# Moving the stick-breaking attention beside the projections, and half of the output projection between the latent units

## The reference, cut to what matters

```python
h = rms_norm(x, g_pre_mix[i])
proj = h @ w_in[i]
sb_q, sb_k, sb_v, q_lat, kv_lat, k_rope = split(proj)
# stick-breaking: A = sigmoid(z) * prod of (1 - sigmoid(z)) over the keys between, 8 heads of 64
z = einsum('bhqd,bhkd->bhqk', q, k) * scale
log_keep = where(strict, -softplus(z), 0)
log_keep_after = cumsum(log_keep, reverse=True) - log_keep
o_sb = where(strict, exp(log_sigmoid(z) + log_keep_after), 0) @ v
# latent attention (MLA): 8 heads, queries and keys out of 256 and 128 latent features
q = rms_norm(q_lat, g_q_lat[i]) @ w_q_up[i];  kv = rms_norm(kv_lat, g_kv_lat[i]) @ w_kv_up[i]
o_mla = causal softmax attention of (q_nope, rope(q_rope)) on (k_nope, rope(k_rope)), v
mix = concatenate([rms_norm(o_sb, g_grp_sb[i]), rms_norm(o_mla, g_grp_mla[i])]) @ w_o[i]
x = x + rms_norm(mix, g_post_mix[i])
```

## Time and profile before

| | |
|---|---|
| median of three runs | 971.93 us |
| the profiled execution's own time | 972.83 us |
| its span | 971.1 us, 16923 instructions |
| TensorE busy | 893.0 us (92%) |
| VectorE, ScalarE, GpSimd busy | 689.6 (71%), 510.7 (53%), 320.6 us (33%) |
| DMA | 137.18 MB, mean 141 GB/s |
| the chain that ended last | TensorE 77%, VectorE 14%, issue 4%, ScalarE 4%, DMA 1% |

### The profile page before, as it was taken

The page is one execution under the profiler, slowest core; times in us unless marked ns, Lnnn a source line. Parts: engine busy times, 40 slices in busy tenths (PEclk is TensorE's granted clock), DMA queues, the critical chain, the costliest instruction groups (busy, mean ns, idle before and its releaser), DMA issues.

```text
span 971.1 us, 16923 instructions
## 1 busy us (share of the span) xinstructions
PE 893.0 (92%) x6718; PEld 850.5 (88%) x6718; DVE 689.6 (71%) x984; ACT 510.7 (53%) x926; POOL 320.6 (33%) x150
## 2 busy tenths in 40 slices
PE   4996779999999998889999489999996999999998
PEld 4985669999999998788989479988996999999998
DVE  6757742899889993768879998754677476566573
ACT  6377345654555556765756264446643544444441
POOL 4653103122233333253545451221343223223220
PEclk8997869999999998999999798899998999999999
DMA  5734004354565665361655242222354456656651
GB/s 190 280 112 150 22 2 115 107 181 149 168 206 177 204 183 154 91 191 62 208 158 166 111 152 66 87 87 66 101 161 130 125 159 197 187 176 184 189 153 44
DMA packets 54078, 137.18 MB, mean 141 GB/s; under 512 B 6000, under 2 KB 24816, under 8 KB 53872
## 3 DMA queue, kind: packets, MB, share of 16 engines
q1 hardware_dynamic: 54000, 136.11, 45.1%
HBM read 135.03 MB, written 1.05 MB: 140 GB/s over the span
## 4 chain that ended last, share of the span: by engine, by line
PE 77%; DVE 14%; issue 4%; ACT 4%; DMA 1%; SPq 0%; DVEq 0%; ACTq 0%
PE PROD L576 15%; PE PROD L577 14%; PE PROD L578 14%; PE SC L717 3%; PE OP L761 3%; DVE wlo L1491 3%; PE PROD L638 2%; PE OP L576 2%; PE OP L578 2%; PE OP L577 2%; PE SC L576 2%; PE SC L577 2%; PE SC L578 2%; PE TP L578 2%; PE TP L577 2%
## 5 line engine op out<-in xcount | busy, mean ns | idle before, releaser
L559 POOL TENSOR_TENSOR wlo<-raw,whi 128x1024 fp32r<-128x1024 f32 x124 | 316.7, 2561 | 626.8 <-ACT whi L1012 626.8
L576 PE MATMUL PROD<-HA,whi 128*128 128x256 f32 x1096 | 318.5, 291 | 10.4 <-DVE HA L1519 5.7
L577 PE MATMUL PROD<-HA,wlo 128*128 128x256 f32 x1096 | 314.3, 287 | 0.0
L578 PE MATMUL PROD<-HA,whi 128*128 128x256 f32 x1096 | 314.1, 287 | 0.0
L1012 ACT ACTIVATE whi<-raw 128x1024 fp32r<-128x1024 f32 x252 | 261.4, 1050 | 45.6 <-PE PROD L578 24.2
L1491 DVE TENSOR_TENSOR wlo<-raw,whi 128x1024 fp32r<-128x1024 f32 x128 | 183.1, 1434 | 102.9 <-ACT whi L1012 102.6
L576 PEld LDWEIGHTS PROD<-HA,whi 128*128 128x128 f32 x1096 | 214.8, 196 | 13.0 <-DVE HA L1519 6.1
L577 PEld LDWEIGHTS PROD<-HA,wlo 128*128 128x128 f32 x1096 | 214.9, 196 | 0.6 <-issue 0.6
L578 PEld LDWEIGHTS PROD<-HA,whi 128*128 128x128 f32 x1096 | 214.6, 196 | 0.0
L1906 DVE SCALAR_TENSOR_TENSOR CY<-U,CV,CY 128x255 f32<-128x255 f32 (+29 forms) x120 | 71.5, 670 | 0.2
L1773 DVE SCALAR_TENSOR_TENSOR YC<-Y,CV,YC 128x255 f32<-128x255 f32 x88 | 66.9, 763 | 2.2 <-ACT YC L1206 0.7
(11 more groups left out here) (316 smaller groups left out, 1707.7 us busy)
## 6 DMA issues: line engine op xcount, KB each, us to landing
raw<-stream SPq DMA_DIRECT2D x208, 512.0 KB, 3.9
raw<-stream SPq DMA_DIRECT2D x136, 128.0 KB, 2.4
raw<-stream SPq DMA_DIRECT2D x8, 384.0 KB, 3.1
raw<-stream SPq DMA_DIRECT2D x8, 256.0 KB, 3.3
X<-xT SPq DMA_DIRECT2D x2, 512.0 KB, 5.1
E<-memT SPq DMA_DIRECT2D x1, 1024.0 KB, 5.8
out<-X SPq DMA_DIRECT2D x8, 128.0 KB, 2.0
PX<-pT SPq DMA_DIRECT2D x1, 256.0 KB, 3.8
```

Source lines behind the costliest of these rows:

```text
L559: nc.gpsimd.tensor_tensor(wlo[:, n % NSPLIT, :], raw[:, n % NRAW, :], whi[:, n % NSPLIT, :].bitcast(F32), ALU.subtract).then_inc(lo_pool, 1)
L576: nc.tensor.matmul(dst, wh, hi, start=start, stop=False, skip_group_check=True)
L577: nc.tensor.matmul(dst, wl, hi, start=False, stop=False, skip_group_check=True)
L578: last = nc.tensor.matmul(dst, wh, lo, start=False, stop=stop, skip_group_check=True)
```

## The change

The first latent stage and its neighbours are put in another order.

- `mem` is loaded by two DMAs into `KMEM` and `VMEM` instead of one into `E0`, so that `E0` is free earlier.
- TensorE runs `sb_scores(0)` to `(2)` after `sbk` 1 to 3 and `sb_scores(3)` a quarter into `sbv`; `sb_cum` after every second `qup`; `sb_pv` behind it, the last one after `kup`. `scores(mla 0)` stands before `vup`. In the latent loop `scores(u+1)` stands before `turn(u)` and `pv(u)`.
- ACT runs the exponentials and logarithms of the stick-breaking units around the norm of `mem`, ahead of the splits of tiles 18 to 21. `token_root(osb)` stands between `exps(mla 0)` and `exps(mla 1)`.
- VectorE's stream follows this (`sb_scaled`, `softplus`, `sb_argument`, `rope_queries` are old code under names).
- The first six outputs of `wo` are computed in two halves: chunks 0 to 3 (the stick-breaking half) two outputs at a time after `pv` of latent units 1, 2 and 3, and chunks 4 to 7 after `turn_out(omla)`. Six outputs share the three banks, two in each, and the stream's order of blocks follows; each of these tiles is then loaded by two DMAs.

```diff
 for _n, _k, _m, _o in STAGES:
-    if _n in ("up", "up2"):
+    if _n == "wo":
+        for _h in (0, 4):
+            ORDER += [FIRST["wo"] + m * 8 + k for m in range(6) for k in range(_h, _h + 4)]
+        ORDER += range(FIRST["wo"] + 48, FIRST["wo"] + 64)
+    elif _n in ("up", "up2"):
...
+WO_HALVES = 6
...
     if _o[0] in ("down", "down2"):
         _k = 4 + _o[1] // 2
+    elif _o[0] == "wo" and _o[1] < WO_HALVES:
+        _k = _o[1] // 2
+        _seen[_k] = _i
+        PREV[_o] = _last.get(_k) if _o[1] % 2 == 0 else None
+        _last[_k] = _o
     else:
...
-T_USES = [("cum", 0)]
-for _u in range(1, 4):
-    T_USES += [("cum", _u), ("mla", _u - 1)]
-T_USES += [("mla", 3), ("osb", 0), ("omla", 0), ("mem", 0), ("mem", 1), ("omem", 0)]
+T_USES = [("cum", u) for u in range(4)] + [("mla", 0), ("osb", 0)] + [("mla", u) for u in range(1, 4)]
...
-O_USES = [("sb", 0), ("mla", 0), ("sb", 1), ("mla", 1), ("sb", 2), ("mla", 2), ("sb", 3), ("mla", 3)]
+O_USES = [("sb", u) for u in range(4)] + [("mla", u) for u in range(4)]
...
-        MEMX = E0[:, :, :].rearrange("p h n -> p (h n)")[:, 0:DC * S].rearrange("p (c s) -> p c s", c=DC)
+        MEMX = [KMEM[:, :, :], VMEM[:, :, :].rearrange("p q n -> p (q n)").rearrange("p (c s) -> p c s", c=4)]
...
+            if o[0] == "wo" and o[1] < WO_HALVES:
+                return PROD[:, k, o[1] % 2 * S:o[1] % 2 * S + S]
...
                 if n == 6:
-                    sp.dma_start(MEMX, memT).then_inc(mem_in, 16)
+                    for i in range(2):
+                        sp.dma_start(MEMX[i], memT[:, 4 * i:4 * i + 4, :]).then_inc(mem_in, 16)
...
             for m in range(4):
                 fm("sbk", m, HA)
+                if m:
+                    wait_freed(pe, ("sbk", m - 1))
+                    sb_scores(m - 1)
             stat("mem", [SQ[:, c, :] for c in range(8)])
-            tm("sbv", 512, HA)
+            tm("sbv", 512, HA, ks=range(0, 2))
+            wait_freed(pe, ("sbk", 3))
+            sb_scores(3)
+            tm("sbv", 512, HA, ks=range(2, 8))
             for m in range(8):
                 fm("qup", m, HL, SP0["ql"] if m == 0 else None)
-                if m == 1:
-                    wait_freed(pe, ("sbk", 3))
                 if m % 2:
-                    sb_scores(m // 2)
+                    sb_cum(m // 2)
+                    if m > 1:
+                        sb_pv(m // 2 - 1)
+            sb_pv(3)
+
+            def wo_half(m, h):
+                dst = begin(("wo", m)) if h == 0 else product(("wo", m))
+                for c in range(4 * h, 4 * h + 4):
+                    if m == 0:
+                        pe.wait_ge(a_lo, SP0["o"] + c + 1)
+                    blk3(dst, FIRST["wo"] + m * 8 + c, HA[:, c, 0:S], HA[:, c, S:2 * S],
+                         c == 0 and m % 2 == 0, c == 7, c == 7)
+
+            wait_freed(pe, ("kup", 3))
+            pe.wait_ge(qm_ready, 1)
+            scores(("mla", 0))
             tm("vup", 512, HL, base=2)
+            pe.wait_ge(qm_ready, 2)
             for u in range(4):
-                sb_cum(u)
-                if u:
-                    sb_pv(u - 1)
-                    turn(("mla", u - 1), PR1)
+                if u < 3:
+                    scores(("mla", u + 1))
+                turn(("mla", u), PR1)
+                if u == 0:
+                    wait_freed(pe, ("vup", 1))
+                pv(("mla", u))
+                if u == 0:
+                    turn_out(("osb", 0), OSB, o_normed, 2)
                 else:
-                    wait_freed(pe, ("vup", 1))
-                scores(("mla", u))
-                if u:
-                    pv(("mla", u - 1))
-            sb_pv(3)
-            turn(("mla", 3), PR1)
-            pv(("mla", 3))
-            turn_out(("osb", 0), OSB, o_normed, 2)
+                    wo_half(2 * u - 2, 0), wo_half(2 * u - 1, 0)
             turn_out(("omla", 0), OMLA, o_normed, 4)
-            for m in range(8):
-                fm("wo", m, HA, SP0["o"] if m == 0 else None)
+            for m in range(WO_HALVES):
+                wo_half(m, 1)
+            for m in range(WO_HALVES, 8):
+                fm("wo", m, HA)
             stat("postmix", [SQ[:, c, :] for c in range(8)])
 
...
-                wait_product(act, ("down", m | 1) if o[0] == "down" else o)
+                pair = o[0] == "down" or o[0] == "wo" and m < WO_HALVES
+                wait_product(act, (o[0], m | 1) if pair else o)
...
-                    nc.scalar.activation(E0[:, 4:6, 0:S], src[:, qt, :].rearrange("p (c s) -> p c s", c=2), ACT.Square,
+                    nc.scalar.activation(Z[:, 4:6, 0:S], src[:, qt, :].rearrange("p (c s) -> p c s", c=2), ACT.Square,
...
+            def sb_weights(u):
+
+                act.wait_ge(sb_arg, u + 1)
+                z = Z[:, 2 * u:2 * u + 2, :]
+                nc.scalar.activation(z, z, ACT.Exp).then_inc(sb_a, 1)
+
+            act.wait_ge(a_lo, SP0["kvl"] + 1)
+            act.wait_ge(mem_in, 32)
+            for c in range(8):
+                squares("mem", c, MEMX[c // 4][:, c % 4, :])
+                if c % 2 and c < 7:
+                    copy_out(("sbk", 1 + c // 2), KS1[:, 1 + c // 2, :])
+            root("mem", D)
+            warm(ACT.Exp)
+            sb_exp(0)
+            sb_exp(1)
+            normed_high(HB, "mem", 8, "norm_mem_2")
+            sb_exp(2)
+            sb_exp(3)
+            act.wait_ge(sb_e, 4)
+            for u in range(4):
+                e = E0[:, 2 * u:2 * u + 2, :]
+                nc.scalar.activation(e, e, ACT.Ln, bias=1.0).then_inc(sb_l, 1)
+            warm(ACT.Exp)
+            for o in (("sbk", 3), ("sbv", 1)):
+                ahead(o)
             for h in range(HEADS):
                 copy_out(("qup", h), QM[:, h, :])
                 if h in (3, 5, 7):
-                    sb_exp(h // 2 - 1)
+                    sb_weights(h // 2 - 1)
             for m in range(4):
                 if m == 2:
-                    sb_exp(3)
+                    sb_weights(3)
                 o = ("kup", m)
                 wait_product(act, o)
                 nc.scalar.activation(KM[0:64, 2 * m, :], product(o)[0:64, 0:S], ACT.Copy)
                 nc.scalar.activation(KM[0:64, 2 * m + 1, :], product(o)[64:128, 0:S], ACT.Copy).then_inc(free(o), 1)
                 ahead(o)
-            act.wait_ge(sb_e, 4)
-            for u in range(4):
-                e = E0[:, 2 * u:2 * u + 2, :]
-                nc.scalar.activation(e, e, ACT.Ln, bias=1.0).then_inc(sb_l, 1)
+            scale_mla = (DH + ROPE) ** -0.5
+            exps(("mla", 0), PR1, scale_mla)
+            act.wait_ge(o_free, OU[("sb", 3)] + 1)
+            token_root("osb", 0, OSB)
             warm(ACT.Exp)
             ahead(("vup", 1))
-            scale_mla = (DH + ROPE) ** -0.5
-            for u in range(4):
-                act.wait_ge(sb_arg, u + 1)
-                z = Z[:, 2 * u:2 * u + 2, :]
-                nc.scalar.activation(z, z, ACT.Exp).then_inc(sb_a, 1)
-                exps(("mla", u), PR1, scale_mla)
+            exps(("mla", 1), PR1, scale_mla)
+            turned_high(HA, ("osb", 0), "g_grp_sb", 0)
+            exps(("mla", 2), PR1, scale_mla)
+            exps(("mla", 3), PR1, scale_mla)
             warm(ACT.Sqrt)
-            act.wait_ge(o_free, OU[("sb", 3)] + 1)
-            token_root("osb", 0, OSB)
             act.wait_ge(o_free, OU[("mla", 3)] + 1)
             token_root("omla", 1, OMLA)
-            turned_high(HA, ("osb", 0), "g_grp_sb", 0)
+            weights(FIRST["wo"] // BPT + NSPLIT + 2)
             turned_high(HA, ("omla", 0), "g_grp_mla", 4)
             for m in range(8):
                 out_block(("wo", m), m, "g_post_mix")
...
+            def sb_scaled(u):
+                dve.wait_ge(s_ready, u + 1)
...
+            def softplus(u):
                 dve.wait_ge(sb_l, u + 1)
                 e, z = E0[:, 2 * u:2 * u + 2, :], Z[:, 2 * u:2 * u + 2, :]
...
+            def sb_argument(u):
                 dve.wait_ge(t_ready, TU[("cum", u)] + 1)
...
+            def rope_queries(h, t1, t2):
+                wait_freed(dve, ("qup", h + 1)), wait_freed(dve, ("qup", h + 2)), wait_freed(dve, ("qup", h + 3))
...
+                                             ALU.mult))
+                nc.vector.tensor_tensor(q[64:96], t1, t2, ALU.add).then_inc(qm_ready, 1)
+
+            def follow(o):
+                wait_product(dve, o)
+                ahead(o)
+
+            for o in (("sbq", 2), ("sbq", 3), ("sbk", 0), ("sbk", 1)):
+                follow(o)
+            sb_scaled(0)
+            follow(("sbk", 2))
+            sb_scaled(1)
+            follow(("sbk", 3))
+            sb_scaled(2)
+            inverse_root("mem")
+            scaled("mem", MEMX, 8)
+            sb_scaled(3)
+            normed_low(HB, "mem", "mem", 8, "norm_mem_2")
+            for qt in range(QT):
+                copy_out(("sbv", qt), VS1[:, qt, :], 512)
+            softplus(0)
+            softplus(1)
+            sb_argument(0)
```

(29 more changed lines are left out.)

88 lines of the change are left out of this document (23 added, 65 removed).

## The result

Fifteen runs of the changed kernel have a median of 982.61 us (977.36 to 991.17), fifteen of the kernel before beside them 976.80 (967.83 to 986.27). The ratio is **1.0082, 95% interval 1.0052 to 1.0112**: slower by 0.8%, about 8 us (5 to 11). The profiled execution of the changed kernel took 981.73 us.

The account below looks back on a forecast made before the run. TensorE, busy 92% of 971.1 us, was taken as the bound, winnable only where idle or at low clock. Terms -1.7 + 4 (clock) + 1.5 (lock) = +3.8 gave 976.6 or 975.7, stated as 975 us, range 962 to 986.

Parts of the forecast that it names:

- the gap: Before sb_cum(0), TensorE idle from 79.5 to 89.8, 10.3 us, ended by VectorE's softplus: idle time moved forward, not filled.
- `sb_scores(1)` waits for tile 14: Beside the projections, TensorE waits 1.2 us while VectorE finishes tile 14 and scales; the root of mem moves to 66.1.
- ScalarE's unbroken row sets tile 20, and tile 20 ends the gap: From the root of mem, 20.7 us of ScalarE work give tile 20's high part at 86.8; softplus(0) queues behind it.
- The lock, term (b): VectorE's tile 20 and softplus(0) delayed by GpSimd's rests of tiles 18, 19 and 21; bounds 0 and 4.3, taken 1.5 us.
- The units among the up-projections: Stick-breaking units between qup and kup, from sb_cum(0) at 89.8 to scores(mla 0) at 112.9.
- The latent loop and the clock, term (a): Latent units end with turn_out(omla) at 152.0 at full clock; TensorE's low clock after gaps costs 0 to 11, taken 4 us.
- 15.9 us behind the end of `turn_out(omla)`: Rest of wo after the last latent transposes: 15.9 us left instead of 23.5, as half the outputs are partly done.
- Two table loads on the path: In the latent loop, two new ScalarE table loads around token_root(osb) delay exps(1), which could else run at 119.7, to 124.5.
- the count without costs of -1.7: End of wo at 167.9 instead of 169.58 with the full clock and no lock: the change wins 1.7 us.
- the ceiling: Attention part, 81.6 to 145.75: removing all idle time and low clock would win about 26 to 28 us, near 3%.
- The denser rival: Latent stage runs denser than counted, turn_out(omla) ending before 143; 961 us; chance 0.17.
- the rival of a low clock: TensorE stays at 1.2 GHz from 89.8 to about 131, turn_out(osb) ending after about 130; 987 us; chance 0.20.

Follow-up runs that it names:

- `t20_later`: Changed kernel with VectorE's wait for tile 20 moved from ahead of softplus(0) to behind sb_argument(0); 976.45 us, ratio 1.0030 to the kernel before.
- `pool_held`: Changed kernel with GpSimd's rests of tile 18 and later held until softplus(1) is done; 981.47 us, ratio 1.0084 to the kernel before.
- `filled`: Changed kernel plus matmuls whose results are overwritten, 22 ahead of sb_cum(0) and 7 ahead of turn_out(osb); 980.21 us, ratio 1.0065 to the kernel before.
- `interleaved`: Changed kernel with ScalarE's splits of tiles 18 to 20 moved among the exponentials, ahead of the logarithms; 971.88 us, ratio 0.9979 to the kernel before.
- `no_halves`: Changed kernel with wo whole, all eight outputs after turn_out(omla); 984.70 us, ratio 1.0106 to the kernel before.
- `combined`: `interleaved` with sb_exp(0), sb_exp(1) earlier, splits of tiles 18, 19 behind sb_exp(3), tile 24's split and tile 23's rest later; 975.59 us, ratio 1.0017.
- `combined_busy`: `combined` plus overwritten matmuls, 4 ahead of sb_cum(0), 3 ahead of turn_out(osb), 2 ahead of each later pv; 968.15 us, ratio 0.9959 to the kernel before.
- `kept_busy`: `interleaved` with tile 24's split later, plus overwritten matmuls: 10 ahead of sb_cum(0), 3 ahead of turn_out(osb), 2 per later pv; 972.63 us, ratio 0.9968.

## Why the prediction was right

The forecast was 975 us, in effect 3.1 over the median shown, inside 962 to 986, and the likeliest outcome was no change within 1%. The median of 982.61 lies in the range and the change of 0.8% within the 1%. The cause of the gap was right. The size was not: in the attention stage the change cost 12.3 us and not the 3.8 of the sum, and it stayed within 1% partly by luck, since 3.5 us came back in code that it does not touch. By its steps:

- **`sb_scores(1)` waits for tile 14.** 0.90 instead of 1.2; the root of `mem` came at 66.18 for 66.1.
- **ScalarE's unbroken row sets tile 20, and tile 20 ends the gap.** VectorE took up the rest of tile 20 at 86.56 for 86.8, after a wait of 7.7 (said: 7), and `t20_later` shows the cause: without that wait `sb_cum(0)` goes to 82.8.
- **The lock, term (b), was mis-sized.** Taken at 1.5 of 0 to 4.3, it measured 6.6 on the path, over its own upper bound: 0.4 for the rest of tile 20, 2.1 and 2.0 for softplus(0), 2.1 for `token_norm(osb)`. The bound counted two instructions, and the mask of softplus(0) and `token_norm` came on top. The Trainium skill (SBUF — State Buffer, "SBUF: two separate sides") has a VectorE instruction with two SBUF inputs blocked by a GpSimd instruction that reads SBUF and started first, for all of that instruction; the trace agrees, 3.09 for 0.95, and by that rule I would have paid my upper bound. I weighed the rule against one row that did not show it (1.22 at 73.40), though GpSimd was at work from 70.84. The trace of the kernel before resolves that row. The timeline of GpSimd of the kernel before, its second instruction there:

```profile
73.42 3.44 POOL L559 TENSOR_TENSOR wlo<-raw,whi 128x1024 fp32r<-128x1024 f32 x1
```

  It begins 0.02 after VectorE's instruction and takes 3.44 where the next one takes 2.39: VectorE had started on the boundary of two, and GpSimd was the one that waited. So the row was the same lock the other way round and no evidence against it. That `token_norm` could meet tile 24 I had not seen.
- **The units among the up-projections.** 24.2 instead of 23.1 from `sb_cum(0)` to `scores(mla 0)`.
- **The latent loop and the clock, term (a).** From `turn_out(osb)` to `turn_out(omla)` my count at the full clock was 26.9. It took 32.7; the excess of 5.8 is over the 4 that I took for all of the stage and within 0 to 11. Executions with the same code in this stretch took 29.98 (`pool_held`) and 30.04 (`t20_later`) at a clock of 0.89, 31.62 (`filled`) at 0.84, 32.74 at 0.80 and 33.76 (`interleaved`) at 0.75: the lower the clock, the longer. So against an execution at 0.89 the clock of this one cost some 3 of the 5.8. The other 3 are my count and what 0.89 costs against the full clock, and no run with this code separates them; with the matmuls that lead nowhere the stretch took 29.1 at 0.95, still 2.2 over the count.
- **15.9 us behind the end of `turn_out(omla)`.** 17.13 from its start to the end of `wo`, 1.1 of them its own: 16.0.
- **Two table loads on the path.** This was wrong. In the changed kernel `exps(1)`, which stands behind them, ends with the first of these rows (ScalarE), and TensorE comes to `scores(2)`, which waits for it, some 3.5 us later (second row, TensorE), after `turn_out(osb)`:

```profile
129.88 0.37 ACT L1103 ACTIVATE Y<-SC,mx 128x128 f32<-128x128 f32 x1
...
133.86 1.06 PE L729 MATMUL SC<-KM,QM 96*128 96x256 f32 x2
```

  In `no_halves`, where `token_norm(osb)` met no lock, the two come together at 130.0 and 130.1. What TensorE waited for here was VectorE's `token_norm(osb)`, 3.64 us.

Sum: 4.2 at `sb_cum(0)`, 1.1, 2.7 to `turn_out(osb)` (2.1 of it the lock), 5.8 and 0.2 are 14.0 over the count without costs of -1.7, which gives +12.3 in the stage; 3.5 came back in the second block, in unchanged code. So `turn_out(omla)`, which the prediction put at 151 to 158, came at 164.8. The median passed 981.6, from which the prediction called it slower, because the kernel before was slower too: 976.80 beside it for the 971.93 that the 1% was taken from. One sum in the prediction is off: 20.5 and 3 to 8 more are 23.5 to 28.5 us, not 26 to 28, so the ceiling was 2.4 to 2.9%. The denser rival needed `turn_out(omla)` to end before 143; it began at 164.8. The mark of the rival of a low clock (987), `turn_out(osb)` ending after about 130, was met at 134.1, but not by its mechanism: the units from 94 to 118 ran at 0.92, and of the 9 that `turn_out(osb)` was late on my count, 4.2 were there at `sb_cum(0)` and 2.1 are the lock. What remains open is how much of the 8 us is the lock and how much the clock on an average execution; the runs show each in single profiles only. A lower clock over the whole execution is not what makes the changed kernel slower: the mean over its fifteen is 0.953, and over the executions of the kernel before in the four sessions of the experiments 0.946 to 0.949.

## What to carry to other kernels

A call that means "prepare what is needed later" stands in program order like any other: before moving a chain across it, look what it waits for, on every engine that has it. Here a chain that was put early stood behind such a call, and the gap that it should have closed only moved. And where two engines lock each other out, holding one back moved the delay to the next instructions (`pool_held`, `combined`); what took it off the path was doing the one engine's work while the other had nothing to do (`interleaved`).

## What the runs showed of the hardware

- An instruction of VectorE from SBUF to SBUF with a single tensor input is delayed too: `token_norm(osb)`, two instructions, 2.95 us when GpSimd began 0.08 us before it and 0.88 when GpSimd began 0.5 after it. An instruction that reads PSUM was not: the scaling of `Z` out of the scores took 0.96 at 75.20 and at 77.68 in the kernel before, inside GpSimd's 73.42 to 82.54, and the argument, with one input in PSUM and one in SBUF, 0.96 at 94.06 in `pool_held`, inside GpSimd's 91.93 to 101.59.
- It goes both ways: GpSimd's 128x1024 instruction took 3.44 us where VectorE had begun 0.02 before it, and 2.34 to 2.42 where none of VectorE's was in its way.
- Executions of one kernel differ as their mean granted clock does. The changed kernel took 977.36 us at 0.962 and 991.17 at 0.943; the kernel before, in the session of `combined`, 966.27 at 0.959 and 986.35 at 0.934. That is some 6 to 8 us for each 0.01, in every kernel with twelve executions or more but `combined_busy` (4). What sets the clock of an execution is not shown.
- Unchanged code of VectorE differs by 6.3 us between two executions (17.49 and 11.21) where GpSimd works beside it in both; that it is the same lock is a reading.
- Matmuls that lead nowhere did not help where the wait behind them was still long: in `filled` 9.7 us of them, ended 5.0 us before `sb_cum(0)`, left it as slow as without them (3.4 us), and so did four of them, ended 3.2 us before it, in `combined_busy` (3.2). In `kept_busy`, ended 0.8 us before it, they brought it to 1.8.
